# A hybrid decoder layer on eight cores: padded bias rows, loads in a chain, an opening without f32 matmuls, a new priority list

## The reference, cut to what matters

```
a = rmsnorm(h, norm_mix);  z = a @ w_in          # u | v_g | q | k | v_m | o | i_gate | f_gate
u = gelu(u);  vg = layernorm(gelu(v_g), gm_ln_g, gm_ln_b)
y_gm = u * (tril(w_s) @ vg + b_s)                # 4 heads, chunks of 128 positions
y_ml = sigmoid(o) * rmsnorm(mlstm(q, k, v_m, gates, state))
h = h + concat(y_gm, y_ml) @ w_out
h = h + square(relu(rmsnorm(h, norm_ffn) @ w_up)) @ w_down      # 4096 wide
h = h + sigmoid(rmsnorm(h, norm_ple) @ w_ple_gate) * (p @ w_ple_proj)
y = rmsnorm(h, norm_final)
```

## Time and profile before

| | |
|---|---|
| three runs | 1003.32, 935.01, 1051.42 us; median 1003.32 |
| profiled execution | 938.75 us |
| its span (first to last instruction, core 1, the slowest) | 937.0 us |
| spans of the eight cores | 929.0 to 937.0 us |
| PE busy | 901.1 us (96%), 6012 matmuls |
| DVE, ACT, POOL busy | 549.9, 410.5, 201.1 us |
| HBM read, written | 80.66, 18.12 MB |

### The profile page before, as it was taken

The page is one execution under the profiler, slowest core; times in us unless marked ns, Lnnn a source line. Parts: engine busy times, 40 slices in busy tenths (PEclk is TensorE's granted clock), DMA queues, the critical chain, the costliest instruction groups (busy, mean ns, idle before and its releaser), DMA issues.

```text
span 937.0 us, 17365 instructions; the slowest of 8 cores (929.0 to 937.0 us)
## 1 busy us (share of the span) xinstructions
PE 901.1 (96%) x6012; PEld 539.7 (58%) x6012; DVE 549.9 (59%) x1083; ACT 410.5 (44%) x795; POOL 201.1 (21%) x314
## 2 busy tenths in 40 slices
PE   6999999999999984999999999999999999999995
PEld 3477676678667652555564555555555555555552
DVE  4757678646776773465544444454555465676676
ACT  3677565667675664252121221112211355455454
POOL 3333423414141642020000000020010111112121
PEclk9899999999999998899999999999999999999998
DMA  8992222024000799400136000391112701111112
GB/s 188 212 182 40 91 91 91 14 92 68 1 1 2 123 203 234 71 23 24 45 59 111 12 1 1 49 193 53 45 51 28 150 35 57 51 51 63 45 46 90
DMA packets 25239, 70.00 MB, mean 75 GB/s; under 512 B 2221, under 2 KB 4433, under 8 KB 23618
## 3 DMA queue, kind: packets, MB, share of 16 engines
q0 software_dynamic: 13888, 34.61, 21.9%
q1 hardware_dynamic: 11266, 34.29, 10.4%
HBM read 80.66 MB, written 18.12 MB: 105 GB/s over the span
## 4 chain that ended last, share of the span: by engine, by line
PE 91%; DMA 6%; DVE 1%; issue 1%; POOL 0%; ACT 0%; POOLq 0%; DVEq 0%; ACTq 0%
PE pb L252 91%; DMA AR<-w_down 4%; DMA AR<-rpk 1%; DVE AR L252 1%; POOL AR L276 0%; POOL CPK L276 0%; ACT AR L252 0%; POOLq L283 0%; POOL SMALL L252 0%; DVEq L235 0%; ACTq L283 0%; POOLq L235 0%; ACTq L235 0%; POOLq L620 0%
## 5 line engine op out<-in xcount | busy, mean ns | idle before, releaser
L252 PE MATMUL pb<-AR 128*128 128x512 bf16 (+5 forms) x5298 | 866.5, 321 | 16.4 <-DMA AR<-w_down 13.0
L252 PEld LDWEIGHTS pb<-AR 128*128 128x128 bf16 (+1 forms) x5298 | 493.4, 99 | 355.5 <-issue 31.4
L252 ACT ACTIVATE AR<-pb 128x384 f32<-128x384 f32 (+6 forms) x375 | 178.0, 489 | 403.7 <-PE pb L252 344.7
L252 DVE TENSOR_TENSOR AR<-AR,pb 128x512 f32<-128x512 f32 (+3 forms) x226 | 132.7, 591 | 148.9 <-PE pb L252 148.2
L252 DVE TENSOR_TENSOR AR<-AR 128x384 bf16<-128x384 f32 (+7 forms) x253 | 129.3, 515 | 105.8 <-ACT AR L252 101.6
L252 ACT ACTIVATE AR<-AR 128x128 f32<-128x128 f32 (+5 forms) x171 | 111.0, 680 | 63.0 <-DVE AR L252 48.0
L252 DVE TENSOR_TENSOR AR<-pb,CPK 128x1024 bf16<-128x1024 bf16 (+2 forms) x69 | 73.3, 1072 | 31.5 <-PE pb L252 31.2
L252 POOL TENSOR_TENSOR SMALL<-SMALL,NEGH 128x1 f32<-128x1 f32 (+1 forms) x102 | 70.0, 689 | 57.6 <-DVE SMALL L252 47.1
L252 ACT ACTIVATE AR<-AR,SMALL 128x1024 bf16<-128x1024 f32 (+1 forms) x68 | 70.8, 1057 | 16.8 <-POOL SMALL L252 9.1
L252 POOL TENSOR_SCALAR SMALL<-SMALL 128x1 f32<-128x1 f32 x85 | 22.4, 264 | 231.6 <-ACT AR L252 188.5
L252 DVE TENSOR_TENSOR AR<-pb,AR 128x512 bf16<-128x512 f32 (+3 forms) x87 | 48.5, 582 | 40.0 <-PE pb L252 38.4
(11 more groups left out here) (68 smaller groups left out, 198.6 us busy)
## 6 DMA issues: line engine op xcount, KB each, us to landing
AR<-w_up POOLq DMA_DIRECT2D x8, 1024.0 KB, 12.8
AR<-w_down POOLq DMA_DIRECT2D x8, 1024.0 KB, 25.8
y_p<-AR SPq DMA_DIRECT2D x16, 512.0 KB, 2.7
hscr<-AR SPq DMA_DIRECT2D x8, 512.0 KB, 2.7
AR<-xp SPq DMA_DIRECT2D x4, 1024.0 KB, 6.8
AR<-hscr SPq DMA_DIRECT2D x8, 512.0 KB, 12.5
AR<-sC SPq DMA_DIRECT2D x8, 512.0 KB, 5.8
o_Cs<-AR SPq DMA_DIRECT2D x8, 512.0 KB, 6.1
```

Of the source, the lines that this page charges most:

```text
L252: ins = getattr(e, name)(**kw)
```

## The change

- `BL` and `BSR` are cleared to 128 rows at the start and the bias matmuls take all 128; rows 9 to 127 are zero.
- The opening has no f32 matmuls: the layer norm's gain and shift come to all partitions by transfers (`gln`, `partition_broadcast`), and the rows for the bias factors come ready, nine rows high (`rpk`), so that `thirds` starts from them. The sample tile's bias row does the same.
- The first x tile is issued by SP instead of POOL; on POOL, x of G1 and G2 are moved ahead; `w_m` and x of G3 wait for the first norm of G0 instead of the second.
- The loads of the first two FFN quarters, the parked residuals and the first states form a chain: q0's four halves in turn (in the scheduler alone), the eight `hscr` reloads after q0 (a wait on the chip), q1 after the first issued reload (a wait on the chip), `sC` after q1 (a wait on the chip). Transfers without a group get ranks ahead of all else.
- The last tile's last stage goes by halves of 512 columns, with the norm's square sum in two parts.
- `MOVES` is another table.

```diff
@@ due
-                o.rank = -1e3 + o.idx * 1e-3 if o.tag == "start" else 1e4 + o.idx
+                o.rank = -1e3 + o.idx * 1e-3 if o.tag == "start" or o.dma else 1e4 + o.idx
@@ MOVES
-B1 -123.2  B2/pe 37.8  B2 -144.8  B3/pe 6.1  B3/act 16.8  B3/dve 41.6  B3 28.4  BN2 51.1  BN3/pe -45.5  BN3 46.9
+B0/act 4.6  B0 -41  B2/pe 12.8  B3/pe 5  B3 57.5  BN0 -66.2  BN1 -27.5  BN2 -250.5  BN3 -143.1  BN5 -259  C/pe 55
...
@@ start
+        load_x(GROUPS[0], one=True)
         dma(CPK[:, 0:192], cpk[:, 0:192], eng="pool")
-        load_x(GROUPS[0], eng="pool", one=True)
-        for i in range(2):
-            dma(WU2[i].rearrange("p k n -> p (k n)"), w_u2[i], eng="pool")
+        dma(rp, rpk[:, 0:2, :], eng="pool")
+        dma(WU2[0].rearrange("p k n -> p (k n)"), w_u2[0], eng="pool")
+        load_x(GROUPS[1], eng="pool")
+        dma(WU2[1].rearrange("p k n -> p (k n)"), w_u2[1], eng="pool")
         dma(CPK[:, 192:512], cpk[:, 192:512], eng="pool")
-        row_load()
         ws_load(0, BIG[0], "pool")
-        load_x(GROUPS[1], eng="pool")
+        dma(GROW, gln[0].partition_broadcast(128), eng="pool")
+        load_x(GROUPS[2], eng="pool")
         load_win("v")
-        load_x(GROUPS[2], eng="pool")
+        memset("dve", BSR, 0.0)
+        memset("dve", BL, 0.0)
+        thirds(rp[:, 0, :], BL[0:9, :], 58)
-        def row_consts():
-            for i, r_ in enumerate((GROW, BROW)):
-                p = ps("M")
-                mm(p, [(ONEF[0:1, :], rp[:, i * 512:(i + 1) * 512])])
-                cp("act", r_, p)
...
@@ bias_rows
-            mmx([(p[0:9, :], SELB[:, 0:9], WM[:, ty].rearrange("p h t -> p (h t)"), True, False),
-                 (p[0:9, :], SEL1[0:1, 0:9], row, False, True)])
-            thirds(p[0:9, :], BSR[0:9, ty, :], 61)
+            mmx([(p[0:9, :], SELB[:, 0:9], WM[:, ty].rearrange("p h t -> p (h t)"), True, True)])
+            tt("dve", row, p[0:9, :], row, ALU.add)
+            thirds(row, BSR[0:9, ty, :], 61)
@@ stage_V
-                     (pm[:, h, :], BL[0:9, hs_[h]], BSR[0:9, ty, hs_[h]], False, True)
+                     (pm[:, h, :], BL[:, hs_[h]], BSR[:, ty, hs_[h]], False, True)
@@ state_load, load_q
-            dma(CSF[c % 3], sC[h, :, half * 8:half * 8 + 8, :])
+            dma(CSF[c % 3], sC[h, :, half * 8:half * 8 + 8, :], after=q1[3:])
+            for a, b in zip(r, r[1:]):
+                b.preds.add(a.idx)
+            return r
@@ stage_C, for the last tile
+                if last:
+                    stt("dve", hsl[:, cs], tc_[:, cs], 0.5, hsl[:, cs], ALU.mult, ALU.add)
+                    act(ABC[par][:, cs], hsl[:, cs], AF.Square, scale=1.0 / 32, accum=small(n, 40 + nn, 1))
+            if last:
+                rs, tmp = small(n, 43, 1), small(n, 42, 1)
+                stt("dve", tmp, small(n, 40, 1), small(n, 41, 1), EPSC[:], ALU.add, ALU.add)
+                tt("pool", rs, tmp, NEGH[:, 0:1], ALU.pow)
+                lo, hi = slice(0, 512), slice(512, 1024)
+                tt("pool", tc_[:, hi], hsl[:, hi], NF[:, hi], ALU.mult)
+                stt("dve", tc_[:, lo], hsl[:, lo], rs, NF[:, lo], ALU.mult, ALU.mult)
+                act(tc_[:, hi], tc_[:, hi], AF.Copy, scale=rs)
+                for cs in (lo, hi):
+                    dma(t["y"][:, cs], tc_[:, cs])
+                return
@@ after the mixing stage
-        load_q(0)
-        load_q(1)
+        q0 = load_q(0)
...
+        back_h = [dma(Hs(t), hscr[t["n"]], after=q0[3:]) for tg in TG for t in tg if not t["kept"]]
+        q1 = load_q(1, back_h[-1:])
```

More of the change, by code:

```diff
@@ new lines @@
+#1245 15.9  #1285 3.7  #1328 -3.5  #1330 16.6  #1338 -12.7  #1344 7  #1351 -13.2  #1357 2.9  #1359 -3.8  #1383 -2.9
+#1408 13  #1423 -4.3  #1484 3.3  #1544 -5.8  #1575 -3.2  #1577 -10.8  #1634 -40.5  #1659 33.6  #1677 12.6
+#1719 35.3  #1739 16.6  #1850 -56.9  #1856 -17.4  #2373 67.3  #2542 32.6  #2668 -26.5  #2670 22.3  #2696 -18
+#2700 -10  #2720 22.2  #2746 50  #2755 19.6  #2776 -12.3  #2802 59.8  #2830 6.7  #2860 33.6  #2868 35.4  #2884 51.5
+#2892 -24.3  #2914 2  #2932 -22.6  #2953 11.2  #2988 45.7  #2990 -31.2  #2996 13.6  #3012 -33.9  #3016 -75
@@ L607 @@
+#3044 -15.7
 """
@@ L850, in build @@
         SELB = A.bf(16)
-        SEL1 = A.f32(32)
         AT[3] = A.bf(8 * 256, k8(8))
@@ L945, in load_x, with thirds @@
             dma(AR[:, o_:o_ + DM * len(grp)], xs if t["ty"] else xp[t["i"] // 2], eng, after=af)
-        rp = AR[0:1, NUM[0].offset:NUM[0].offset + 2048]
-        def row_load():
-            dma(rp, rpk, eng="pool")
+        rp = AR[0:9, NUM[0].offset:NUM[0].offset + 1024].rearrange("p (a n) -> p a n", a=2)
+        def thirds(p, out, mcol):
+            q = QTD[0].rearrange("p j t -> p (j t)")
+            c1, r1, c2 = q[0:9, 0:512], QCSS.rearrange("p h e -> p (h e)")[0:9, 0:512], q[0:9, 512:1024]
+            cp("dve", c1, p)
+            tt("dve", r1, p, c1, ALU.subtract)
+            cp("dve", c2, r1)
+            tt("dve", r1, r1, c2, ALU.subtract)
+            ts("dve", r1, r1, CPK[0:9, mcol + 2:mcol + 3], ALU.mult)
+            stt("dve", r1, c2, CPK[0:9, mcol + 1:mcol + 2], r1, ALU.mult, ALU.add)
+            stt("dve", out, c1, CPK[0:9, mcol:mcol + 1], r1, ALU.mult, ALU.add)
         def ws_load(ty, t0, eng, af=()):
@@ L1205, in sample_prep @@
             o_ = QTD[1].offset // 2
-            row = AR[0:1, o_:o_ + 512]
-            dma(row, rpk[:, 1536:2048], after=af)
+            row = AR[0:9, o_:o_ + 512]
+            dma(row, rpk[:, 2, :], after=af)
+            dma(BROW, gln[1].partition_broadcast(128), after=af)
             bias_rows(1, row)
@@ L1366, in build, with stage_C @@
         cn = [0]
-        def stage_C(t):
+        def stage_C(t, last=False):
             n = cn[0]
@@ L1407, in front @@
             if gi == 0:
-                row_consts()
-                bias_cols()
                 mix_consts(0, BIG[0], BIG[1][:, 0, :])
-                bias_rows(0, rp[:, 1024:1536])
-                load_win("m", after=nops[0][1:])
-                load_x(GROUPS[3], nops[0][1:], "pool")
+                bias_rows(0, rp[:, 1, :])
+                load_x(GROUPS[3], nops[0][:1], "pool")
+                load_win("m", after=nops[0][:1])
             if gi == 1:
@@ L1449, in norm_B @@
             for j, t in enumerate(TG[k]):
-                if not t["kept"]:
-                    dma(Hs(t), hscr[t["n"]])
                 norm_T(t["n"], 44, Hs(t), AB[t["n"] % 2], A2T[k][:, :, j * 128:(j + 1) * 128], G_FFN)
@@ L1553 @@
     bs = f(gm_bs)[0]
-    rpk = np.concatenate([f(gm_ln_g)[0], f(gm_ln_b)[0], bs.reshape(512), np.tile(bs[:, :8], (1, 16)).reshape(512)]).reshape(1, 2048)
+    rpk = np.zeros((9, 3, 512), np.float32)
+    rpk[0:3, 0], rpk[3:9, 0] = 1.0, f(gm_ln_b)[0]
+    rpk[0:3, 1], rpk[0:3, 2] = bs.reshape(512), np.tile(bs[:, :8], (1, 16)).reshape(512)
     wt = f(gm_ws)[0].transpose(0, 2, 1)
@@ L1561 @@
                   **{f"w_down{i}": rows(wdn[i * 1024:(i + 1) * 1024]) for i in range(4)},
-                  w_pg=rows(f(w_ple_gate)[0]), w_pp=rows(f(w_ple_proj)[0]), cpk=cpk, rpk=f(rpk), cseg=cseg, nfin=f(norm_final), wsT=f(wsT))
+                  w_pg=rows(f(w_ple_gate)[0]), w_pp=rows(f(w_ple_proj)[0]), cpk=cpk, rpk=rpk, gln=np.stack([f(gm_ln_g)[0], f(gm_ln_b)[0]]), cseg=cseg, nfin=f(norm_final), wsT=f(wsT))
     in_maps = []
```

65 lines of the change are left out of this document (20 added, 45 removed).

## The result

| | before | after |
|---|---|---|
| runs | 1003.32, 935.01, 1051.42, 937.6 | 901.72, 901.3, 901.58, 902.47 |
| median | 970.46 us | 901.65 us |
| profiled execution | 938.75 us | 901.72 us |
| its span | 937.0 (core 1) | 899.8 (core 6) |

The forecast, 899 against 938.75, is a ratio of 0.958; the time lies 2.7 us above it and inside the range. The two profiled executions differ by 37.0 us, where 39.8 were forecast. As the experiments show, that closeness owes much to errors of opposite sign.

What follows compares the result with a forecast made beforehand. PE, 91% of the last chain, bounds the kernel through idle time and work below its rate. 938.75 - 13.9 (padding) - 1.0 (sample row) - 8.9 (opening) - 15 (boundary) - 0.5 (last tile) = 899.4, said 899; range 889 to 916.

Steps and rivals of the forecast that it cites:

- Padding: V's bias matmuls: groups of eight go from 1.275 to 0.447 us with 128 rows, 13.9 us less over 17 tiles.
- rival 3: Bias matmuls: row count doesn't matter, alternation costs the time, so padding gives 0: 913 us; chance 0.07 shared with another rival.
- Opening: Start up to 41 us: offset between wall clock and useful PE work falls from 31.9 to 23.0, 8.9 us less.
- Rival 1: Opening: bound by the loads alone, PE waits at each weight, 9 us given back: 908; chance 0.17 shared with another rival.
- sample tile's bias row: Sample tile: a bf16 and f32 pair becomes one bf16 matmul, 1.0 us less, between 0 and 1.3.
- Boundary: Start of the FFN: w_down wait shrinks to 0 to 2 us, half clock goes; 5 of 20 us left, minus 15.
- Last tile by halves: Chain behind the last matmul: half steps overlap, 0.5 us gained, between -0.5 and 1.5.
- Priority list: New order on all engines: taken as 0, with a bound of 8 us lost.
- The worst case of my sum: Whole kernel: the terms' bounds moved together the bad way, without a rival, give 916.7 us.
- 2: Rival at the FFN boundary: w_down wait stays at half, half clock returns: 911; chance 0.17 shared with another rival.
- 4: Rival at the boundary: POOL's w_up1 issue waits, PE stands behind it, 50 us lost: 944, slower; chance of slower 0.03.
- 5: Rival: q0's chain has no chip wait, costing nothing; if the reloads' wait is also ineffective, 914; chance 0.07 shared.

## Why the prediction was right or wrong

**Padding: right.** 13.9 forecast, 14.0 by undoing it, 0.90 us for two groups. With equal columns, order and clock, the rows alone make the difference, and rival 3 fell. In the trace of before, the starts of the 16 matmuls of the earlier trace rows follow each other at 0.15 to 0.16 us throughout, the full ones like the 9-row ones. The Trainium skill ("TensorE: Matmul & The Clock Gate", Step-by-step: what each phase is for) says of the weight load alone that the row count K doesn't matter; the step from there to a padding worth 0 was the rival's, and it doesn't hold where 9 and 128 rows alternate. Why the alternation is slow is not shown: no run put the four 9-row matmuls one behind the other, which would tell the cost of 9 rows from that of the change between 9 and 128.

**Opening: right in sign, too large.** By the same count as in the forecast the offset went from 31.9 to 24.6, where I said 23.0, and 1.9 us more were lost by 80 us: 5.4 in place of 8.9. The start slipped, which I hadn't priced: the first constants stand behind nothing on POOL but are in flight together with x, now issued by SP, and landed near 9.2 us; the first transposes moved from 12.0 to 15.85. But putting them first gained nothing, so the slip is not what bounds it. The step that failed is the bound: I bounded the stage by w_k alone, and PE was held at 32.17 by the x of the third group (21.65 us in flight) and its norm, and, with that hold taken away, by w_m (1.88 us) for a gain of 0.9 at most. Several loads in turn bind. Rival 1 had the right kind of cause (the loads bind) with too high a price. The 1.0 us for the sample tile's bias row is in no row and no run by itself.

**Boundary: right in place, mis-sized, and its reason wrong.** I forecast 5 of 20 us left; about 0.7 are (0.26 idle and two fillers), so about 19 gained instead of 15. I gave the credit to the chain. The chip waits are worth 0 (901.49), and the chain as a whole 7 us (908.36), as on the old kernel (7.5). The small gaps of 320 to 361, which I left in place, are gone, and three of five fillers with them; PE's order is another there. The loads are too: before, two halves of w_up1 (321.75, 325.72) and two of w_down (330.12, 334.64) were issued within 13 us and were in flight together; now w_down's halves stand alone, at 302.7 and 318.1. Of the forecast steps, "the second w_down half is issued near 311" was 7 us early, "the first down-projection stands near 323" likewise, and the two errors cancelled.

**Last tile by halves: wrong sign.** I forecast 0.5 us gained and it costs 1.9 behind the last matmul. The step that failed: I priced the half steps by themselves and gave POOL's product no price. It stretched the step that DVE ran beside it from 1.28 to 2.23 us, and the eps step, whose place behind that one I had seen, inherited the delay. The Trainium skill ("SBUF — State Buffer", SBUF: two separate sides) says that a DVE operation with two SBUF inputs and a GpSimd operation that reads SBUF lock each other out for a whole instruction. The rows agree: POOL's product ends at 892.25, and 1.28 us later would be 893.53, where DVE's step ends at 893.33 (POOL's spans are rough to some tenths).

**Priority list: the step that failed most.** I took 0: "PE has no idle time from 41 to 320 us before, so it can only lose here." (The worst case of my sum doesn't hold the 8 us that I gave as its bound either.) That compared the new list with the old order. The right comparison is with the new code without a list, and it says 25 us. Going from the padded and chained old kernel (918.4) to the changed one (901.5) the sum reads: new opening and tail without lists +6.4 (920.5 to 926.9), new list in place of the old -23 (25.4 against 2.1). By place the terms nearly close: 14.0 + 1.0 (not shown) + 5.4 + 18.7 - 1.7 = 37.4, where the two spans differ by 37.2. By edit they don't. I booked opening and boundary by what a good order would allow, and took for granted that PE stays without idle time from 41 to 320 us. Without its list the changed kernel has 9.2 us of waits and 22 fillers there, and 15 fillers at the boundary, though the w_down wait is gone without it too. So the forecast came near by luck, in part: what the terms "opening 8.9" and "boundary 15" promise comes through only with a list that stood in the sum at 0, and an opening and a tail priced too well met a boundary priced too low.

**Rivals.** 1: cause seen, price not. 2: no w_down wait at all. 3: fell. 4: the wait at w_up1's issue exists (16.3 us), but only with the old order, and PE has no idle time while POOL stands there; its step from POOL's wait to one of PE fell. 5: true to the letter, the chip waits do nothing, and harmless, since the order of the queues is enough.

**What stays open.** How much of the 17 us between 918.4 and 901.5 the new opening would give with a list made for it alone: list and opening were not separable, as a table by number fits only its own code. Whether the product alone or the second store alone makes the 1.8 us in the tail was not tried; the step on DVE gives 0.95 of it. Before's wait for w_down differs from core to core (7.9 to 13.2 us), and the slowest cores have the longest; what makes the loads of one core slower than those of another is not known.

## What to carry to other kernels

Ask of a scheduler's priority table what the code is worth without it, on both sides of a change: comparing two tuned orders by their idle time shows 0 for a table that is worth 25 us. When a wait for a load is removed, look at where the loads are issued and in what company before crediting a semaphore: here the waits on the chip were worth nothing, and the chain in the scheduler, which orders PE's work along with the loads, 7 us. A wait on a side engine costs only if PE stands for it: read PE's rows at the same time before giving it a price. A side engine that is idle is not free while another engine reads and writes the same memory beside it; price the neighbour's step as well.
